# Down products in another order, with weight tiles made early and POOL left to begin transfers

## The chip, the cores and the metric

The kernel runs on one core of one Trainium2 chip. The metric is the device time of one execution in microseconds (us). TensorE is PE in the rows, VectorE DVE, ScalarE ACT, GpSimd POOL, and SyncE SP, which here only begins transfers.

## The reference, cut to what matters

Two blocks run one after the other on a 512 x 1024 activation; the change touches only the end of the second, its MLP and the final norm:

```python
u = _rmsnorm(h, mlp_norm_g[l])
h = h + jnp.square(jax.nn.relu(u @ w_up[l])) @ w_down[l]
...
h = _rmsnorm(h, final_norm_g)
return h[:, N_META:]
```

`w_up` is 1024 x 4096, `w_down` 4096 x 1024, all in float32.

## The kernel before

Each float32 operand is split into a high and a low half (`a_high` and `a_low` for activations, `hi` and `lo`), and PE sums high times high, low times high and high times low. ACT makes the high half of a weight tile (`cast`, a copy), DVE or POOL the low half (`w_low` on DVE, `low` on POOL, a subtraction each).

The MLP is cut into four parts of 1024 hidden columns. A part first has eight up tiles, each 24 matmuls on PE. The down product of the part is a Strassen-Winograd scheme: seven products instead of eight, named `P11`, `P_7`, `P_5`, `P12`, `P_6`, `P_3`, `P_4`, in the order of the numbers that the line `P11, P_7, ... = range(7)` gives them. Each takes an activation operand (a quarter or a signed sum of quarters, `x_sums`), and a weight operand (a quarter of `w_down` or a signed sum). Each weight operand has two tiles, h = 0 and 1; the fourteen tiles of a part are counted by i = 2n + h, n the product's number. The weight sums are made in `w12_w22` (`w_w` in the rows): SP loads a quarter, POOL begins DMA transfers that add further rows of `w_down` from DRAM (`w_sum`, `accum_op=ALU.add`): two tiles each for `P_7`, `P_5` and `P_6`, where the sum for `P_6` is put on top of that for `P_5`, and so begins only when the low halves of the two tiles of `P_5` are made. DVE adds the last term for `P_4` (`w_sum4`). The weights `w22`, one quarter without a sum, belong to `P_3`.

Every product fills two PSUM banks (r = 0, 1: rows 0 to 127 and 128 to 255 of an activation half), DVE empties them (`out`, in the last part `last_out`), and `down_free` says which emptying PE waits for before it fills banks again. `P_3` and `P_4` stay in PSUM over the parts. In the last part the sums over the products are spread over `OT`, the 512 x 1024 result in four row blocks, of which `y_half(1, 1)` (called y22) is the lower right quarter. Then the norm: ACT squares with a row sum (`square`), DVE makes mean and reciprocal, ACT the root, and DVE (`scale_left`) and ACT (`scale_right`) multiply; `times_g` multiplies by the gain `gl`. Each result block is stored as soon as it is scaled.

Each engine runs its list in the order in which its program writes it, and waits on semaphores only; the lists are written by hand. `raw` holds the weights as loaded for all tiles up to the last up tile. In the last part POOL makes the low halves of five second tiles (`P_5`, `P12`, `P_6`, `P_3`, `P_4`, h = 1) and, at the very end, finishes y22 and multiplies two blocks by the gain.

## Time and profile before

| what | us |
|---|---|
| median of 3 runs (1005.85 to 1006.09) | 1006.0 |
| the profiled execution | 1006.45 |
| its span, first to last instruction | 1004.7 |
| PE busy in the span | 983.4 |
| DVE busy in the span | 625.3 |
| POOL busy in the span | 552.3 |

The profile shows one execution. Busy time of PE counts overlapped matmuls; where the next matmul follows with no idle time in a timeline row, PE does not wait. A timeline row gives start, duration, engine, line and operation, what is written from what, how many instructions are merged, and in square brackets the idle time ahead and what ended it. Consecutive instructions of DVE overlap a little, so the distance of starts is what one costs.

### The profile page before, as it was taken

To read this page: it belongs to the slowest core of one execution; us is meant where nothing else is said; L and a number is where in the kernel's file an instruction comes from. 1 tells how busy PE (TensorE), PEld (TensorE's weight loads), DVE (VectorE), ACT (ScalarE), POOL (GpSimd) and SP (SyncE) were. 2 spreads that over 40 slices of the span, in tenths; PEclk is the share of its full clock that TensorE was granted. 3 is DMA by queue.
4 is the path that set the end of the run, shared out by engine and by line. 5 is a ranking of instruction groups with operands and counts; after the bars stand their busy time and mean duration, and the time that the engine had idled before them with its cause. 6 is when DMAs were issued, how large, how long until landed. Compare 5 with 4: busy or idle time off the path is not lost.

```text
span 1004.7 us, 12754 instructions
## 1 busy us (share of the span) xinstructions
PE 983.4 (98%) x4859; PEld 830.3 (83%) x4859; DVE 625.3 (62%) x943; ACT 471.8 (47%) x743; POOL 552.3 (55%) x643
## 2 busy tenths in 40 slices
PE   9999999999999999999999999999999999999993
PEld 7888788888888888888899987888888888888882
DVE  5781257665273753454669999773942852685698
ACT  4553345554672223533235775455633443453453
POOL 4555455565565884654657878455074055037084
PEclk9999999999999999999999999999999999999997
DMA  7323221212452225422232212568467458356122
GB/s 233 107 79 114 84 85 52 75 43 84 125 169 84 84 84 191 127 84 84 64 98 92 85 63 84 169 223 195 126 216 161 126 175 202 106 150 136 28 42 84
DMA packets 93276, 115.92 MB, mean 115 GB/s; under 512 B 3954, under 2 KB 70160, under 8 KB 93216
## 3 DMA queue, kind: packets, MB, share of 16 engines
q1 hardware_dynamic: 86384, 102.26, 31.3%
q0 software_dynamic: 6528, 12.58, 7.6%
q8 instruction: 38, 0.62, 0.3%
q10 hardware_dynamic: 304, 0.27, 0.1%
q14 instruction: 22, 0.18, 0.1%
HBM read 113.01 MB, written 2.10 MB: 115 GB/s over the span
## 4 chain that ended last, share of the span: by engine, by line
PE 87%; DVE 9%; ACT 2%; issue 2%; DVEq 0%; ACTq 0%
PE ps L565 63%; PE ps L958 12%; PE ps L584 4%; PE ps L710 1%; PE ps L634 1%; PE ps L731 1%; DVE Hl L1587 1%; PE ps L695 1%; PE ps L694 1%; PE ps L772 1%; PE ps L617 1%; DVE Fm L2334 0%; DVE Fm L2303 0%; DVE X L2389 0%; DVE tmp L2084 0%
## 5 line engine op out<-in xcount | busy, mean ns | idle before, releaser
L2470 POOL TENSOR_TENSOR wlo<-raw,whi 128x256 fp32r<-128x256 f32 x496 | 401.6, 860 | 215.4 <-ACT whi L1014 215.3
L565 PE MATMUL ps<-Hh,whi 128*128 128x512 f32 x512 | 201.8, 394 | 0.7 <-DVE Hl L1587 0.7
L565 PE MATMUL ps<-Hl,whi 128*128 128x512 f32 x512 | 199.6, 390 | 0.0
L1014 ACT ACTIVATE whi<-raw 128x1024 fp32r<-128x1024 f32 (+1 forms) x126 | 132.3, 1050 | 93.8 <-PE ps L565 54.0
L565 PE MATMUL ps<-Ah,whi 128*128 128x512 f32 (+1 forms) x496 | 165.3, 360 | 0.2 <-DVE Al L2238 0.2
L565 PE MATMUL ps<-Al,whi 128*128 128x512 f32 (+1 forms) x496 | 163.7, 356 | 0.0
L565 PE MATMUL ps<-Hh,wlo 128*128 128x512 f32 x512 | 129.3, 389 | 0.3 <-POOL wlo L2470 0.3
L565 PEld LDWEIGHTS ps<-Hh,whi 128*128 128x128 f32 x512 | 96.1, 188 | 20.9 <-DVE Hl L1587 1.5
L565 PEld LDWEIGHTS ps<-Hh,wlo 128*128 128x128 f32 x512 | 96.0, 188 | 20.7 <-POOL wlo L2470 0.7
L565 PEld LDWEIGHTS ps<-Hl,whi 128*128 128x128 f32 x512 | 96.2, 188 | 19.2
L565 PE MATMUL ps<-Ah,wlo 128*128 128x512 f32 (+1 forms) x496 | 104.7, 356 | 0.0
L565 PEld LDWEIGHTS ps<-Ah,whi 128*128 128x128 f32 x496 | 88.0, 188 | 13.7 <-DVE Al L2238 0.8
L565 PEld LDWEIGHTS ps<-Al,whi 128*128 128x128 f32 x496 | 87.9, 188 | 12.7
L565 PEld LDWEIGHTS ps<-Ah,wlo 128*128 128x128 f32 x496 | 83.3, 188 | 13.4
L2511 POOL DMA_DIRECT2D w_w<-in_w_down x20 | 24.3, 1217 | 117.1 <-DVE w_more L1587 53.0
L2270 DVE SCALAR_TENSOR_TENSOR X<-ps,Rb 128x512 f32<-128x512 f32 x32 | 21.8, 689 | 94.1 <-PE ps L565 93.3
L2481 POOL TENSOR_TENSOR P<-P,sm 128x1024 f32<-128x1024 f32 (+1 forms) x16 | 26.9, 1680 | 53.4 <-DVE sm L1779 53.4
L958 PE MATMUL ps<-whi,Hl 128*128 128x512 f32 x216 | 53.8, 390 | 0.1
L1590 DVE TENSOR_TENSOR tmp<-ps,Rb 128x512 f32<-128x512 f32 x25 | 17.2, 689 | 55.6 <-PE ps L565 55.6
L565 PE MATMUL ps<-Ah,w_more 128*128 128x512 f32 x160 | 50.2, 389 | 0.0
L958 PEld LDWEIGHTS ps<-whi,Hl 128*128 128x128 f32 x216 | 40.3, 188 | 9.4 <-issue 0.8
L2470 POOL TENSOR_TENSOR w_more<-raw,w_more 128x256 fp32r<-128x256 f32 x40 | 30.4, 925 | 18.0 <-ACT w_more L1014 18.0
(372 smaller groups left out, 1692.8 us busy)
## 6 DMA issues: line engine op xcount, KB each, us to landing
raw<-in_w_in SPq DMA_DIRECT2D x29, 1024.0 KB, 5.3
raw<-in_w_up SPq DMA_DIRECT2D x16, 1024.0 KB, 5.4
w_w<-in_w_down POOLq DMA_DIRECT2D x20, 512.0 KB, 5.8
Fm<-in_w_down SPq DMA_DIRECT2D x8, 1024.0 KB, 5.1
raw<-in_w_in SPq DMA_DIRECT2D x14, 512.0 KB, 3.7
raw<-in_w_att_out SPq DMA_DIRECT2D x4, 1024.0 KB, 5.1
raw<-in_w_sg_out SPq DMA_DIRECT2D x4, 1024.0 KB, 5.2
raw<-in_w_o SPq DMA_DIRECT2D x4, 1024.0 KB, 5.1
```

The costliest lines, as they stand in the source:

```text
L565: mm = e.matmul(ps[:, bk, 0:c1 - c0], of(j)[:, k % kk, 128 * g:128 * g + 128], x[:, k, c0:c1], start=(start and n == 0), stop=(stop and n ...
L584: mm = e.matmul(ps[:, banks[r], :], x[:, k, 128 * r:128 * r + 128], of(j)[:, k % 2], start=(i == 0 and n == 0), stop=(i == 3 and n == 5))
L617: e.matmul(ps[:, 2, 0:128], ones[:], ones[:], start=True, stop=True)
L634: mm = e.matmul(ps[:, i, :], of(i)[:, k], x[:, k], start=(k == 0 and of is w_hi and x is Hh), stop=last)
L694: e.matmul(out, lhs, kdh[:, g, k0:k0 + W], start=True, stop=False)
L958: mm = e.matmul(ps[:, down_bank(part, n, r), :], x[:, k, 128 * r:128 * r + 128], of(j)[:, k % 2], start=(first and not (kept and part)), s ...
L1014: return e.activation(out, src, ACT.Copy, scale=scale)
L1590: e.tensor_tensor(out, ps[:, bk, :], R, ALU.mult).then_inc(*b.done("drained", j))
L2270: e.scalar_tensor_tensor(X[:, n], ps[:, up_bank(part, n), :], 0.0, RB, ALU.max, ALU.mult).then_inc(*b.done("drained", j))
L2470: ins = e.tensor_tensor(w_lo(j)[:, *cut], raw_tile(j)[:, *cut], f(w_hi(j))[:, *cut], ALU.subtract)
L2481: e.tensor_tensor(Pf[:, u, :, :, 0:W], Pf[:, u, :, :, 0:W], rb, ALU.mult).then_inc(*b.done("probs", i))
L2511: e.dma_start(w_sum3[h] if n == P_7 else quarter(0, 1, h), src, accum_op=ALU.add).then_inc(*b.done(w_sum_name(n, h), (part, n), 16))
```

## The change

The numbers of `P12` and `P_5` are exchanged, in all four parts, and with them the order of their products on PE and of their tiles. In DVE's program the pieces between are put in another order. `raw` is allocated among the buffers of the first phases, and the new `w_last` over the same bytes: it holds high and low halves of the two tiles of `P_3` in the last part, which ACT and DVE now make while the last up tiles run. POOL makes no low half in the last down part: DVE makes all of them. `w_sum4` of the last part's second tile becomes an adding transfer that POOL begins, and so does the last addition on y22, from SBUF to SBUF. The multiplications by the gain of rows 256 to 511 (right half) go to DVE, and the left half of rows 0 to 255 is multiplied by gain and root in one instruction.

```diff
-P11, P_7, P_5, P12, P_6, P_3, P_4 = range(7)
+P11, P_7, P12, P_5, P_6, P_3, P_4 = range(7)
...
-        raw = sb("raw", [128, 2, 8, 256])
...
+            raw = first.enter_context(nc.sbuf_tensor("raw", [128, 2, 8, 256], F32))
...
+        w_last = sb("w_last", [128, 2, 2, 1024], R32)
...
+        def in_w_last(j):
+            return tiles[j][0] is None and tiles[j][1][:2] == (3, P_3)
+
+        def turn_of(j):
+            m = j - J_UP - 8
+            return m - 2 if j >= down_tile(3, P_4, 0) else m
+
         def w_place(part, j):
-            m = j - J_UP - 8
-            w = (whi, wlo)[part][:, (j if m < 0 else J_UP + 6 + m % 5) % 3].rearrange("p k n -> p (k n)")
-            if m >= 0 and m % 5 < 2:
+            m = turn_of(j)
+            if in_w_last(j):
+                w = w_last[:, tiles[j][1][2], part]
+            elif m >= 0 and m % 5 < 2:
                 w = w_more[:, m % 5, part]
+            else:
+                w = (whi, wlo)[part][:, (j if m < 0 else J_UP + 6 + m % 5) % 3].rearrange("p k n -> p (k n)")
...
-            if tiles[j][0] is not None:
-                return "lo", j
-            part, n, h = tiles[j][1]
-            return ("lo" if part == 3 and n >= P_5 and h == 1 else "w_low"), j
+            return ("w_low" if tiles[j][0] is None else "lo"), j
...
+                if n == P12 and part == 3:
                     return "first_kept", r
-                return "down_out", (part, {P_5: P11, P12: P_7, P_6: P_5}[n], r)
+                return "down_out", (part, {P12: P11, P_5: P_7, P_6: P12}[n], r)
...
                     else:
-                        w.wait_ge(*(("w_sum4", (part, h)) if n == P_4 else (w_sum_name(n, h), (part, n))))
-                m = j - J_UP - 8
-                before = j - 5 if m >= 2 else j - 3
-                if m in (0, 1):
+                        by_dve = n == P_4 and (part, h) != (3, 1)
+                        w.wait_ge(*(("w_sum4", (part, h)) if by_dve else (w_sum_name(n, h), (part, n))))
+                m = turn_of(j)
+                before = j - 3 if m < 2 else j - 5 if m == j - J_UP - 8 else j - 7
+                if in_w_last(j):
+                    w.wait_ge("lo", J_UP + 22 * 3 + 7)
+                elif m in (0, 1):
                     w.wait_ge("residual_turned", 7)
...
+                        if (part, n) == (3, 6):
+                            for h in range(2):
+                                cast(down_tile(3, P_3, h))
...
-                    if j < n_tiles:
+                    if i == 6:
+                        a_high(part, P_3)
+                    if i == 8:
+                        a_high(part, P_4)
+                    if j < n_tiles and not in_w_last(j):
                         cast(j)
-                    for n in {1: (P_5,), 2: (P12,), 4: (P_6,), 7: (P_3,), 8: (P_4,)}.get(i, ()):
-                        a_high(part, n)
-                    if part == 3 and i == 3:
+                    if i in (0, 2, 3):
+                        a_high(part, {0: P12, 2: P_5, 3: P_6}[i])
+                    if part == 3 and i == 2:
                         for r in range(2):
                             w.wait_ge("down_out", (3, P11, r))
...
-                if low_ready(j)[0] == "lo":
-                    return
...
+                b.value["vector_step", ("last", n)] = b.count["vector_step"]
...
                     if n == 6:
-                        for i in range(4):
+                        for i in (0, 1, 2, 3) if part < 3 else (0, 1, 2, 3, 10, 11):
                             w_low(part, i)
                 x_sums(part, P_5)
                 w_low(part, 4)
+                a_low(part, P12)
+                w_low(part, 5)
+                if part < 3:
+                    out(part, P11)
+                else:
+                    last_out(P11)
+                w_low(part, 6)
                 a_low(part, P_5)
-                w_low(part, 5)
-                send(P11)
                 x_sums(part, P_6)
-                w_low(part, 6)
-                a_low(part, P12)
-                send(P_7)
                 w_low(part, 7)
+                if part < 3:
+                    out(part, P_7)
+                else:
+                    last_out(P_7)
                 a_low(part, P_6)
                 w_low(part, 8)
                 x_sums(part, P_3)
                 w_sum4(part, 0)
-                send(P_5)
-                w_low(part, 9)
-                w_sum4(part, 1)
-                a_low(part, P_3)
-                w_low(part, 10)
-                w_low(part, 11)
-                w_low(part, 12)
-                a_low(part, P_4)
-                w_low(part, 13)
-                send(P12)
-                send(P_6)
+                if part < 3:
+                    out(part, P12)
+                    a_low(part, P_3)
+                    w_low(part, 9)
+                    w_sum4(part, 1)
+                    w_low(part, 10)
+                    w_low(part, 11)
+                    w_low(part, 12)
+                    a_low(part, P_4)
+                    w_low(part, 13)
+                    out(part, P_5)
+                    out(part, P_6)
+                else:
+                    last_out(P12)
+                    a_low(part, P_3)
+                    w_low(part, 9)
+                    w_low(part, 12)
+                    last_out(P_5)
+                    a_low(part, P_4)
+                    w_low(part, 13)
+                    last_out(P_6)
...
+                y = Z[:, r, 0:cut]
                 w.wait_ge("final_factor", r)
-                w.wait_ge(*(("first_times", r) if r < 2 else ("y22_times", r)))
-                w.wait_ge("last_times", r)
-                e.tensor_scalar(Z[:, r, 0:cut], Z[:, r, 0:cut], R4[:, r:r + 1], None, ALU.mult).then_inc(
-                    *b.done("scaled_left", r))
+                if r < 2:
+                    w.wait_ge("down_out", (3, P12, r))
+                    w.wait_ge("a_low", (3, P_4))
+                    e.scalar_tensor_tensor(y, OT[:, r, 0:cut], R4[:, r:r + 1], gl[:, 0:cut], ALU.mult, ALU.mult).then_inc(
+                        *b.done("scaled_left", r))
+                else:
+                    w.wait_ge("first_times", r)
+                    w.wait_ge("last_times", r)
+                    e.tensor_scalar(y, y, R4[:, r:r + 1], None, ALU.mult).then_inc(*b.done("scaled_left", r))
...
             w.wait_ge("down_out", (3, P_6, 1))
             add(y_half(0, 1), acc[3])
             add(y_half(1, 0), acc[3], ALU.subtract)
             w.wait_ge("final_g_in", 0)
-            for r in range(2):
-                times_g(r, 0, 512, "first_times", r)
+            w.wait_ge("a_low", (3, P_4))
             for r in range(2):
                 last_add(r, 0, down_bank(3, P_3, r), 512, 512)
-            for r in range(4):
+            for r in range(2):
                 first_mean(r)
             for r in range(2):
                 last_mean(r, 0)
             for r in range(2):
                 scale_left(r)
+            w.wait_ge("y22_set", 0)
+            for r in range(2, 4):
+                times_g(r, 512, 512, "first_times", r)
             last_add(2, 0, 6, 0, 512)
+            for r in range(2, 4):
+                first_mean(r)
             last_mean(2, 0)
             scale_left(2)
             last_add(3, 0, 7, 0, 256)
             add(OT[:, 3, 256:512], ps[:, 7, 256:512])
             last_mean(3, 0)
-            last_add(3, 1, down_bank(3, P12, 0), 256, 256)
+            last_add(3, 1, down_bank(3, P_5, 0), 256, 256)
             last_mean(3, 1)
             scale_left(3)
...
-                q, r = {P_7: (1, 1), P_5: (0, 0), P_6: (1, 1)}[n]
+                q, r = {P_7: (1, 1), P_5: (0, 0), P_6: (1, 1), P_4: (1, 0)}[n]
                 if n == P_7:
                     w.wait_ge("quarter7_in", (part, 1))
                 elif n == P_5:
                     w.wait_ge("quarter01_in", part)
                 else:
-                    w.wait_ge(*low_ready(down_tile(part, P_5, h)))
+                    w.wait_ge(*low_ready(down_tile(part, P_5 if n == P_6 else P_6, h)))
                 r0, c0 = 1024 * part + 512 * q + 256 * h, 512 * r
...
-                if part == 3:
-                    low(down_tile(3, P_5, 1))
                 w_sum(part, P_6, 1)
                 if part < 3:
                     lows(up_tile(part + 1, 0), up_tile(part + 1, 5))
-            for n in (P12, P_6, P_3, P_4):
-                low(down_tile(3, n, 1))
-
-            y = y_half(1, 1)
+            w_sum(3, P_4, 1)
             w.wait_ge("down_out", (3, P_6, 1))
-            e.tensor_tensor(y, y, acc[3], ALU.add).then_inc(*b.done("y22_set", 0))
-            w.wait_ge("y22_set", 0)
-            w.wait_ge("final_g_in", 0)
-            w.wait_ge("a_low", (3, P_4))
-            e.tensor_tensor(Z[:, 2, 512:1024], OT[:, 2, 512:1024], gl[:, 512:1024], ALU.mult).then_inc(
-                *b.done("y22_times", 2))
-            e.tensor_tensor(Z[:, 3, 512:1024], OT[:, 3, 512:1024], gl[:, 512:1024], ALU.mult).then_inc(
-                *b.done("y22_times", 3))
+            w.wait_ge("vector_step", ("last", P_5))
+            e.dma_start(y_half(1, 1), acc[3], accum_op=ALU.add).then_inc(*b.done("y22_set", 0, 16))
```

The bank and tile names in the waits of PE are exchanged likewise.

DVE in the first part, from the `out` of `P11` on. Low halves of weights read `hi`'s semaphore, `Hl` and `x_part` are low halves of activations, `tmp<-X` an activation sum, `w_w<-w_w,Fm` is `w_sum4`, and `Fm<-ps` an `out`. Before:

```order
L2314 COPY Fm<-ps 128x512 [waits s_products] x2
L2282 TENSOR_TENSOR tmp<-X,tmp 128x1024 [waits s_all_low]
L1587 TENSOR_TENSOR w_more<-Fm,w_more 128x1024 [waits s_hi]
L1587 TENSOR_TENSOR Hl<-X,Hl 128x1024 [waits s_all_high]
L2314 COPY Fm<-ps 128x512 [waits s_products] x2
L1587 TENSOR_TENSOR wlo<-Fm,whi 128x1024 [waits s_hi]
L1587 TENSOR_TENSOR Hl<-tmp,Hl 128x1024 [waits s_all_high]
L1587 TENSOR_TENSOR wlo<-w_w,whi 128x1024 [waits s_hi]
L2282 TENSOR_TENSOR tmp<-X,tmp 128x1024 [waits s_all_low]
L2292 TENSOR_TENSOR w_w<-w_w,Fm 128x1024 [waits s_all_low,s_quarter10_in]
L2314 COPY Fm<-ps 128x512 [waits s_products] x2
```

And now:

```order
L2331 COPY Fm<-ps 128x512 [waits s_products] x2
L1606 TENSOR_TENSOR w_more<-w_w,w_more 128x1024 [waits s_hi]
L1606 TENSOR_TENSOR Hl<-tmp,Hl 128x1024 [waits s_all_high]
L2301 TENSOR_TENSOR tmp<-X,tmp 128x1024 [waits s_all_low]
L1606 TENSOR_TENSOR wlo<-w_w,whi 128x1024 [waits s_hi]
L2331 COPY Fm<-ps 128x512 [waits s_products] x2
L1606 TENSOR_TENSOR Hl<-tmp,Hl 128x1024 [waits s_all_high]
L1606 TENSOR_TENSOR wlo<-w_w,whi 128x1024 [waits s_hi]
L2301 TENSOR_TENSOR tmp<-X,tmp 128x1024 [waits s_all_low]
L2311 TENSOR_TENSOR w_w<-w_w,Fm 128x1024 [waits s_all_low,s_quarter10_in]
L2334 TENSOR_TENSOR Fm<-ps,Fm 128x512 [waits s_residual_set,s_products]
```

The `out` ahead of the fifth product was that of `P_5`, and is now that of `P12` (the row with `s_residual_set`). The low half of tile 6 now stands right behind the `out` of `P11`: it is the first tile of `P_5`, the one that POOL's transfer for `P_6` waits for, and it was tile 4, above these rows, before.

POOL at the end of the program, before:

```order
L2511 DMA w_w<-in_w_down 128x2x512
L2511 DMA w_w<-in_w_down 128x2x512 [waits s_all_low]
L2470 TENSOR_TENSOR w_more<-w_w,w_more 128x2x128 [waits s_hi]
L2470 TENSOR_TENSOR w_more<-w_w,w_more 128x2x128 x3
L2511 DMA w_w<-in_w_down 128x2x512 [waits s_lo]
L2470 TENSOR_TENSOR wlo<-Fm,whi 128x2x128 [waits s_hi]
L2470 TENSOR_TENSOR wlo<-Fm,whi 128x2x128 x3
L2470 TENSOR_TENSOR w_more<-w_w,w_more 128x2x128 [waits s_hi]
L2470 TENSOR_TENSOR w_more<-w_w,w_more 128x2x128 x3
L2470 TENSOR_TENSOR wlo<-tmp,whi 128x2x128 [waits s_hi]
L2470 TENSOR_TENSOR wlo<-tmp,whi 128x2x128 x3
L2470 TENSOR_TENSOR wlo<-w_w,whi 128x2x128 [waits s_hi]
```

And now:

```order
L2554 DMA w_w<-in_w_down 128x2x512
L2554 DMA w_w<-in_w_down 128x2x512 [waits s_all_low] x3
L2613 DMA Fm<-Fm 128x2x512 [waits s_vector_step,s_down_out]
```

The rows of subtractions (two for each of the five tiles) are gone, and so are the addition and two multiplications behind them. Three adding transfers into `w_w` wait for DVE, and a fourth on `Fm` (y22) waits for the last `out`.

ACT at the end of the program; the first rows are the squares, the order of which the change leaves alone:

```order
L1569 ACTIVATE Fm,sm<-Fm 128x512 [waits s_down_out] x2
L1569 ACTIVATE Fm,sm<-Fm 128x512 [waits s_y22_set]
L1569 ACTIVATE Fm,sm<-Fm 128x512
L1569 ACTIVATE Fm,sm<-Fm 128x512 [waits s_last_added] x2
L1579 ACTIVATE sm<-sm 128x1 [waits s_all_inverse]
L1023 ACTIVATE X<-X,sm 128x512 [waits s_last_times,s_final_factor]
```

The squares of rows 256 to 511 (`s_y22_set`) stand ahead of those of the last-added columns of rows 0 to 255 (`s_last_added`). What sets `y22_set` was POOL's addition, and is now the end of the transfer.

## Rows read from the trace of the kernel before

**Rows 1.** The page, part 1: busy us, share of the span, instructions.

```profile
PE 983.4 (98%) x4859; PEld 830.3 (83%) x4859; DVE 625.3 (62%) x943; ACT 471.8 (47%) x743; POOL 552.3 (55%) x643
```

**Rows 2.** Timeline of PE, first part: start, duration, instruction, idle before.

```profile
725.14 1.07 PE L958 MATMUL ps<-wlo,Hl 128*128 128x512 f32 x4
726.27 2.09 PE L958 MATMUL ps<-whi,Hl 128*128 128x512 f32 x8
```

**Rows 3.** Timeline of DVE, first part.

```profile
709.99 1.22 DVE L1587 TENSOR_TENSOR wlo<-w_w,whi 128x1024 fp32r<-128x1024 f32 x1
...
716.30 1.22 DVE L1587 TENSOR_TENSOR w_more<-Fm,w_more 128x1024 fp32r<-128x1024 f32 x1
717.43 1.22 DVE L1587 TENSOR_TENSOR Hl<-X,Hl 128x1024 fp32r<-128x1024 f32 x1
...
725.44 1.28 DVE L2314 COPY Fm<-ps 128x512 f32<-128x512 f32 x2
```

**Rows 4.** Timeline of ACT, first part.

```profile
717.41 1.06 ACT L1014 ACTIVATE whi<-w_w 128x1024 fp32r<-128x1024 f32 x1 [2.90 <-DMA w_w<-in_w_down]
...
723.50 1.06 ACT L1014 ACTIVATE whi<-w_w 128x1024 fp32r<-128x1024 f32 x1 [4.09 <-DMA w_w<-in_w_down]
```

**Rows 5.** Timeline of POOL, first part, then third part.

```profile
711.62 1.20 POOL L2511 DMA_DIRECT2D w_w<-in_w_down  x1 [12.57 <-DVE wlo L1587]
717.72 1.21 POOL L2511 DMA_DIRECT2D w_w<-in_w_down  x1 [4.90 <-DVE w_more L1587]
...
872.20 1.21 POOL L2511 DMA_DIRECT2D w_w<-in_w_down  x1 [22.61 <-DVE wlo L1587]
879.11 1.22 POOL L2511 DMA_DIRECT2D w_w<-in_w_down  x1 [5.69 <-DVE w_more L1587]
```

**Rows 6.** DMA to landing, us: lines L2511 (POOL, adding), then L497 (SP).

```profile
DMA to landing us min/median/max: 5.5/5.8/6.6
...
DMA to landing us min/median/max: 3.3/4.6/5.5
```

**Rows 7.** Timeline of PE, last part.

```profile
949.44 2.88 PE L958 MATMUL ps<-w_more,Hl 128*128 128x512 f32 x12
...
971.27 2.29 PE L958 MATMUL ps<-whi,Hl 128*128 128x512 f32 x8
...
982.46 1.98 PE L1006 MATMUL ps<-whi,Hl 128*128 128x512 f32 x8
```

**Rows 8.** Timeline of DVE, last part.

```profile
949.64 0.69 DVE L2270 SCALAR_TENSOR_TENSOR X<-ps,Rb 128x512 f32<-128x512 f32 x1 [0.21 <-PE ps L565]
951.03 1.23 DVE L2282 TENSOR_TENSOR tmp<-X 128x1024 f32<-128x1024 f32 x1 [0.70 <-ACT X L1511]
...
975.33 1.76 DVE L1587 TENSOR_TENSOR w_more<-tmp,w_more 128x1024 fp32r<-128x1024 f32 x1
...
982.88 4.56 DVE L2303 TENSOR_TENSOR Fm<-Fm 128x1024 f32<-128x1024 f32 x2
987.48 3.33 DVE L2389 TENSOR_TENSOR X<-Fm,P 128x512 f32<-128x512 f32 x2
990.73 0.68 DVE L2400 TENSOR_TENSOR Fm<-ps,Fm 128x512 f32<-128x512 f32 x1
...
993.38 0.33 DVE L2394 TENSOR_SCALAR sm<-sm 128x1 f32<-128x1 f32 x4
...
995.51 0.68 DVE L2400 TENSOR_TENSOR Fm<-ps,Fm 128x512 f32<-128x512 f32 x1
```

**Rows 9.** Timeline of POOL, last part.

```profile
982.93 3.44 POOL L2574 TENSOR_TENSOR Fm<-Fm 128x1024 f32<-128x1024 f32 x1 [0.47 <-DVE Fm L2327]
```

**Rows 10.** Timeline of ACT, last part.

```profile
991.44 0.63 ACT L1550 ACTIVATE Fm<-Fm 128x512 f32<-128x512 f32 x1 [3.71 <-DVE Fm L2400]
991.98 0.19 ACT L1550 ACTIVATION_READ_ACCUMULATOR Fm<-Fm 128x1 f32 x1
...
1001.59 0.38 ACTq L1578 DMA_DIRECT2D out<-X  x1
```

More of the change, by code:

```diff
@@ L2344, in vector_program @@
             for part in range(4):
-                send = last_out if part == 3 else lambda n, part=part: out(part, n)
                 for n in range(8):
```

12 lines of the change are left out of this document (6 added, 6 removed).

## The prediction

> **What bounds the kernel now.** I read the page's busy times first: PE is busy 983.4 us [rows 1] of a span of 1004.7, so only two things can move the time: a wait of PE, or the stretch after its last matmul. Then PE's timeline around the down products. In the first part the fifth product, `P_6`, should start when the four matmuls of 725.14 are through. One costs (1.98 - 1.07) / 4 = 0.227 us, from eight and from four in a row [rows 2, 7], so that is at 726.05, and it starts at 726.27 [rows 2]: PE already waits 0.22 there, and the eight matmuls behind take 2.09, 0.11 more than the 1.98. DVE's row says for what: the `out` of `P_5`, begun at 725.44 [rows 3]. PE follows it by 0.83. One product costs 24 x 0.227 = 5.44.
>
> In the last part the down products start at 949.44, the fifth at 971.27 and the last stretch at 982.46 [rows 7]; PE ends near 988.2 by the same pitch (12 matmuls of 512 columns, 24 of 256). The span ends at 1004.7, so 16.5 us lie behind PE, and DVE's timeline says why: it begins the last two additions on `OT` at 982.88, the multiplications by the gain at 987.48, and reaches the products of rows 256 to 383 (`last_add(2, ...)`) only at 995.51 [rows 8]. From there to the issue of the last store is 6.08 [rows 10]. The end is DVE's list, up to 995.51 and then in turn with ACT. POOL makes part of its slowness: two additions take 4.56 beside POOL's of 3.44 [rows 8, 9], where an operation of that size costs 1.14 from start to start (716.30 to 717.43 [rows 3]); and subtractions as that of 975.33 take 1.76 instead of 1.22 [rows 8].
>
> **The change: DVE's work.** In the last part DVE gets five low halves more and gives up one `w_sum4`: +4 x 1.14 = 4.6 us, two of them ahead of the last `act`. Without POOL's subtractions it gets back about 0.54 on each of nine operations between 958 and 980, and 2.2 and 2.0 on the two pairs behind 982.88: 9.1 us. Two multiplications by the gain come (POOL's), two are merged into the scaling: 0.1 or so each. If DVE never waited, I count from the start of `act(3, 7)` 17 operations of 1.14, 14 of 0.60, two dependent additions of 1.25, four tail operations in 2.65 (990.73 to 993.38 [rows 8]), four of 0.60 and 2.6 of small ones and steps: 38 us, from 951.6 to 989.6, 5.9 before 995.51. That is what the change could give. I don't expect it, for the new waits.
>
> **The first part.** I walk DVE's new list from 709.99, where both lists have the low half of tile 4. Steps of 1.14 (the `out` pair 1.20): `a_low(P12)`, `w_low(5)`, `out(P11)` at 713.40, `w_low(6)` at 714.60. ACT's halves are there earlier. Before, POOL's first transfer for `P_6` was begun 1.63 after the start of `w_low(4)` (709.99 to 711.62 [rows 3, 5]); now it hangs on `w_low(6)`: 714.60 + 1.63 = 716.23, 4.6 later. What this delay was covered by: `cast(8)`, which started on landing at 717.41, 5.79 after the issue [rows 4, 5], while the tile's low half was made well after. Now `cast(8)` is at 722.02 and takes 1.06, `w_low(8)` is at 723.08, `x_sums(P_3)` and `w_sum4(0)` follow, and `out(P12)` at 726.50. PE waits for that `out`: fifth product at 726.50 + 0.83 = 727.33, 1.28 late instead of 0.22.
>
> The second transfer starts 6.10 after the first (711.62 to 717.72, with its condition met long before [rows 5]), at 722.33, and lands after 5.78 (717.72 to 723.50 [rows 4, 5]) at 728.11. Two ACT copies of about 1.0 (`cast(9)`, `a_high(P_3)`), then on DVE `a_low(P_3)` at 730.15 and only behind it `w_low(9)` at 731.29, through at 732.5. PE wants it after 20 of the product's 24 matmuls: 727.33 + 4.54 = 731.87. It waits 0.7. In all 1.98 instead of 0.33: **+1.6**, and 0.1 for `a_low(P_4)`, further back in the same list: +1.7. PE's time lost here is lost for good.
>
> **Second and third part.** There DVE is not behind at the start of the down products, and the first transfer would be begun at 876.81 instead of 872.20, `w_low(9)` ready near 893.2, wanted at 894.1. Margin 0.9 with a spacing of 6.1, and 0.1 with 6.91, which the third part's own transfers show [rows 5]. I take nothing; the upper bound is 0.8 for each.
>
> **The last part,** in before's clock. `w_low(3)` was through 0.21 ahead of `act(3, 7)` at 949.64; the two early tiles (2.27) push it to 951.62. The `x_sums` (951.03) starts at 953.01 [rows 8]. Then, with ACT's rows as before: `w_low(4)` 954.15, `w_low(6)` 958.77, first transfer 960.40; `last_out(P_7)`'s four operations 963.44, `w_low(8)` 967.25 (landing 966.19 and a copy), `last_out(P12)` 970.66, so PE's fifth product is at 971.49, 0.2 behind 971.27. Second transfer 966.50, landing 972.28, copies, `a_low(P_3)` 974.35, `w_low(9)` 975.49. PE waits for it from 976.03 to 976.80: 0.8. It moves PE's end to 988.9 and does not bound the end by itself. `w_low(9)` releases the third transfer (`w_sum(3, P_4, 1)`): 977.12, landing 982.9, copy, `w_low(13)` 984.0, `last_out(P_6)` 985.15. That releases the fourth, for y22: second operation at 985.75, its 0.68 [rows 8], and the 0.41 that POOL takes from the end of what it waits for to the issue (709.99 + 1.22 to 711.62): 986.84, landing 5.79 later at 992.63.
>
> Behind the wait for y22 on ACT stand four squares of 0.63 [rows 10] that all of DVE's means need: 992.63, 993.26, 993.89, 994.52. DVE has reached the means by 991.7 and waits. Both means and reciprocals stand ahead of `scale_left(0)`: the fourth square's sum is read 0.73 behind its start (991.44 to 991.98 + 0.19 [rows 10]), and two operations of 0.2 bring `scale_left(0)` to 995.65; four DVE operations of 0.60 follow, and `last_add(2, ...)` starts at 998.05, 2.54 behind 995.51. From there the list is the same but for two small means. **+2.5**.
>
> What is unknown here is a transfer from SBUF to SBUF. The adding transfers from DRAM land after 5.5 to 6.6, plain ones of the same 512 KB after 3.3 at the least [rows 6]. These are my bounds; I take 5.8, since it is the same adding operation of the same shape. With 3.3 all of the tail behind y22 comes 2.5 earlier: +0.05 in place of +2.5; with 6.6, +3.3.
>
> The page DMA: Bandwidth & Descriptors of the Trainium skill (its opening section on the chain of events of a transfer) gives about 2.0 us fixed and the bytes by 436 GB/s, and says that most of the fixed part is the receipt from the target memory, HBM the heaviest. By it 512 KB would take 3.2 us. The trace does not agree for adding transfers, whose least is 5.5 [rows 6], and no row here has one without DRAM.
>
> **Sum.** 1.7 + 2.5 = +4.2 on the span of 1004.7: 1008.9. The profiled execution took 1006.45, 1.75 more than its span, and stands 0.45 above the median. On the median: 1006.0 + 4.2 = **1010.2**.
>
> **Rivals.**
> *y22 lands quickly* (3.3): 1.7 + 0.05, 1007.8. For it: no DRAM read, no other transfer then. Against: all 24 adding ones need 5.5 or more. 0.18.
> *Transfers are spaced as in the third part* (6.91): 0.8 more in the first part, 0.8 in the last part's chain, and the thin margins of parts two and three begin to show: 1011.8 and up to 1013.5. For it: row 872.20 to 879.11. Against: loads of SP ran then, and none do in the last part. 0.12.
> *Faster: the chain of transfers does not bind.* Place: first and last part. Four transfers stand in a row in the last part, so each microsecond that one lands earlier gives up to four back, and two in the first part. At 5.1 from issue to landing both losses are gone (first part +0.3, last -0.3), and below it the 5.9 us of DVE come through: 1002 with 4.7, 1000.1 if nothing waits. For it: POOL no longer subtracts beside them. Against: in the first part it didn't either, and they took 5.78. 0.12.
> *Near no change by cover that I don't see* (an ACT copy that finds a gap, DVE's list shorter than walked): 1004 to 1008. 0.08.
>
> **Numbers.** The forecast has 0.50, for 1008.6 to 1011.5. The range, 1005.0 to 1013.5, leaves out the faster case and the far end of the wide spacing. A measurement of this kernel tells 0.2% (2 us) from no change: faster 0.12; same 0.17 (the last case and half of the quick y22); slower 0.71.
>
> **What would show it.** After: PE idle of about 1.2 and 0.7 at the fifth product and its second tile in the first part, and 0.8 in the last; no POOL subtraction behind 932; POOL's four transfers near 962, 968, 979 and 988.5, and 5.7 to 5.9 from each to its reader; an ACT gap of several microseconds that the y22 transfer ends, DVE idle behind it. Wrong: if ACT's squares start within 4 us of the last issue, if PE's first part shows no new wait, or if DVE is busy without a break up to `last_add(2, ...)`.

## Result, and the profile after

| kernel | median us | runs | profiled execution | its span |
|---|---|---|---|---|
| before | 1005.95 (1005.63 to 1006.09) | 7 | 1006.45 | 1004.7 |
| changed | 1009.04 (1008.4 to 1009.86) | 7 | 1009.45 | 1007.7 |

The ratio is 1.0033, with a 95% interval of 1.0024 to 1.0043: the change makes the kernel 3.1 us slower. The forecast was 1010.2, 4.2 slower.

The page, part 1, of the changed kernel answers to [rows 1]:

```profile
PE 983.2 (98%) x4859; PEld 829.6 (82%) x4859; DVE 630.6 (63%) x947; ACT 470.2 (47%) x743; POOL 532.4 (53%) x622
```

PE has the same work as before. DVE has 5.3 us more, POOL 19.9 less: nothing there says slower. The chain that ended last, part 4 of the page, does; the adding transfers, absent from this list before, are on it now:

```profile
PE 83%; DVE 10%; issue 2%; ACT 2%; DMA 2%; SPq 0%; DVEq 0%; POOLq 0%; ACTq 0%
PE ps L573 62%; PE ps L967 9%; PE ps L592 4%; PE ps L718 1%; DVE wlo L1606 1%; DMA w_w<-in_w_down 1%; PE ps L642 1%; PE ps L739 1%; DVE w_more L1606 1%; DVE Hl L1606 1%; PE ps L703 1%; PE ps L702 1%; DMA raw<-in_w_in 1%; PE ps L780 1%; DMA Fm<-Fm 0%
```

**First part.** The timeline of PE answers to [rows 2]. PE now waits for the `out` of `P12` (L2334) and for the low half of tile 9 (L1606):

```profile
724.39 1.07 PE L967 MATMUL ps<-wlo,Hl 128*128 128x512 f32 x4
726.75 2.08 PE L967 MATMUL ps<-whi,Hl 128*128 128x512 f32 x8 [1.29 <-DVE Fm L2334]
728.68 1.08 PE L967 MATMUL ps<-wlo,Hl 128*128 128x512 f32 x4
729.59 1.97 PE L967 MATMUL ps<-whi,Hl 128*128 128x512 f32 x8
731.84 1.21 PE L967 MATMUL ps<-wlo,Hl 128*128 128x512 f32 x4 [0.27 <-DVE wlo L1606]
732.89 2.46 PE L967 MATMUL ps<-w_more,x_part 128*128 128x512 f32 x10
```

Behind each wait stand an ACT copy of a tile that a transfer fills, and the transfer. POOL, then ACT, then DVE, same stretch; they answer to [rows 3 to 5]:

```profile
715.47 1.20 POOL L2554 DMA_DIRECT2D w_w<-in_w_down  x1 [17.06 <-DVE w_more L1606]
721.73 1.21 POOL L2554 DMA_DIRECT2D w_w<-in_w_down  x1 [5.05 <-DVE Hl L1606]
```

```profile
721.42 1.06 ACT L1023 ACTIVATE whi<-w_w 128x1024 fp32r<-128x1024 f32 x1 [2.86 <-DMA w_w<-in_w_down]
727.38 1.06 ACT L1023 ACTIVATE whi<-w_w 128x1024 fp32r<-128x1024 f32 x1 [4.91 <-DMA w_w<-in_w_down]
```

```profile
722.51 1.23 DVE L1606 TENSOR_TENSOR wlo<-w_w,whi 128x1024 fp32r<-128x1024 f32 x1 [1.59 <-ACT whi L1023]
...
725.92 1.28 DVE L2334 TENSOR_TENSOR Fm<-ps,Fm 128x512 f32<-128x512 f32 x2
729.42 1.22 DVE L1606 TENSOR_TENSOR x_part<-tmp,x_part 128x1024 fp32r<-128x1024 f32 x1 [2.22 <-ACT x_part L1023]
```

The reader sees one chain: transfer at 715.47, copy at 721.42 (5.95 later), low half of tile 8, a sum, `w_sum4(0)`, then the `out` that PE waits for. The copy of the next tile is 5.65 behind its own transfer.

**Last part.** The timelines of POOL, ACT and DVE answer to [rows 8 to 10]:

```profile
961.49 1.22 POOL L2554 DMA_DIRECT2D w_w<-in_w_down  x1 [23.92 <-DVE wlo L1606]
967.58 1.22 POOL L2554 DMA_DIRECT2D w_w<-in_w_down  x1 [4.88 <-issue]
978.08 1.21 POOL L2554 DMA_DIRECT2D w_w<-in_w_down  x1 [9.28 <-DVE w_more L1606]
987.58 1.22 POOL L2613 DMA_DIRECT2D Fm<-Fm  x1 [8.29 <-DVE Fm L2344]
```

```profile
983.65 1.06 ACT L1023 ACTIVATE whi<-w_w 128x1024 fp32r<-128x1024 f32 x1 [6.43 <-DMA w_w<-in_w_down]
...
992.62 0.63 ACT L1569 ACTIVATE Fm<-Fm 128x512 f32<-128x512 f32 x1 [6.69 <-DMA Fm<-Fm]
...
1004.59 0.38 ACTq L1597 DMA_DIRECT2D out<-X  x1
```

```profile
954.11 1.23 DVE L2301 TENSOR_TENSOR tmp<-X 128x1024 f32<-128x1024 f32 x1 [0.70 <-ACT X L1523]
...
984.74 1.23 DVE L1606 TENSOR_TENSOR wlo<-w_w,whi 128x1024 fp32r<-128x1024 f32 x1 [2.36 <-ACT whi L1023]
...
987.20 2.48 DVE L2320 TENSOR_TENSOR Fm<-Fm 128x1024 f32<-128x1024 f32 x2
...
994.60 0.16 DVE L2443 SCALAR_TENSOR_TENSOR sm<-sm 128x1 f32<-128x1 f32 x1 [2.01 <-ACT Fm L1569]
...
998.02 0.68 DVE L2433 TENSOR_TENSOR Fm<-ps,Fm 128x512 f32<-128x512 f32 x1
...
999.98 0.16 DVE L2443 SCALAR_TENSOR_TENSOR sm<-sm 128x1 f32<-128x1 f32 x1 [0.42 <-DVE sm L2427]
```

The two additions take 2.48 instead of 4.56 [rows 8], so DVE is faster where POOL is silent, and it gives the time back waiting for ACT, which waits for transfers. The y22 transfer's own entry says how long it took:

```profile
L2613 POOL DMA_DIRECT2D Fm<-Fm x1: 1223/1223/1223, 987.6 to 987.6; - x1
...
DMA to landing us min/median/max: 5.0/5.0/5.0
```

**One yardstick for all kernels.** The rows give four stretches that add up to the path from the first down product to the last issue: A, from PE's `P11` in the first part to `P11` in the last; B, from there to DVE's `x_sums` (954.11 above, 951.03 in [rows 8]); C, from there to `last_add(2, ...)`; D, from there to the last issue.

| kernel | A | B | C | D | sum |
|---|---|---|---|---|---|
| before | 245.15 | 1.59 | 44.48 | 6.08 | 297.30 |
| changed | 247.01 | 3.56 | 43.91 | 6.57 | 301.05 |
| changed, a second profile | 246.59 | 3.56 | 43.90 | 6.56 | 300.61 |

A starts at 704.29 before and at 703.54 after; between profiles of all the kernels below it lies anywhere from 703.0 to 704.4, ahead of the down products. That is why the sum grows by 3.75 and the span by 3.0. C is the stretch where the change could gain, and it hardly moved: 0.6 less, for 2.0 more in B, where DVE makes the two early tiles. The idle times in DVE's rows within C say why. They were 1.43 in sum and are 7.16 (2.36 and 2.01 are the two shown above whole); C without them fell from 43.05 to 36.75. It is 36.7 to 37.2 in every kernel below in which DVE has the same operations in C and POOL is silent, so there C differs by DVE's waits and by little else.

### The profile page after: what moved, and what is told of

The parts are those of the page before. It is cut to its first block, busy times and chain, and to the rows that moved or that the text cites. A ratio compares the mean times of both kernels' runs of the same rounds, so it can differ in the third digit from the quotient of the medians.

```text
span 1007.7 us, 12730 instructions
## 1 busy us (share of the span) xinstructions
PE 983.2 (98%) x4859; PEld 829.6 (82%) x4859; DVE 630.6 (63%) x947; ACT 470.2 (47%) x743; POOL 532.4 (53%) x622
## 4 chain that ended last, share of the span: by engine, by line
PE 83%; DVE 10%; issue 2%; ACT 2%; DMA 2%; SPq 0%; DVEq 0%; POOLq 0%; ACTq 0%
PE ps L573 62%; PE ps L967 9%; PE ps L592 4%; PE ps L718 1%; DVE wlo L1606 1%; DMA w_w<-in_w_down 1%; PE ps L642 1%; PE ps L739 1%; DVE w_more L1606 1%; DVE Hl L1606 1%; PE ps L703 1%; PE ps L702 1%; DMA raw<-in_w_in 1%; PE ps L780 1%; DMA Fm<-Fm 0%
## 5 line engine op out<-in xcount | busy, mean ns | idle before, releaser
L2513 POOL TENSOR_TENSOR w_more<-raw,w_more 128x256 fp32r<-128x256 f32 x40 | 34.5, 994 | 13.5 <-ACT w_more L1023 13.5
```

What stands on the lines that cost most here:

```text
L2513: ins = e.tensor_tensor(w_lo(j)[:, *cut], raw_tile(j)[:, *cut], f(w_hi(j))[:, *cut], ALU.subtract)
```

## Experiments

Twelve experiments in three groups; the kernel before ran beside each group (medians 1005.94, 1006.1 and 1006.17). The stretches are those of one profiled execution each, the medians those of 5 to 11 executions. All compute the whole reference. Edits are against the changed kernel where nothing else is said; the stretches of all of them are in a table at the end of this section.

### Two causes in the tail

`squares_first`: ACT squares the last-added columns of rows 0 to 255 and scales them ahead of the two squares that need y22 (`first_square(r)` stands for the wait and the square of one row block).

```diff
-            for r in range(4):
+            for r in range(2):
                 first_square(r)
             for r in range(2):
                 last_square(r, 0, 512, 512)
             for r in range(2):
                 scale_right(r)
+            for r in range(2, 4):
+                first_square(r)
```

> The changed kernel with ScalarE's squares of the last-added columns of rows 0 to 255, their roots and scalings put ahead of the two squares that wait for the y22 transfer. If that wait is what holds VectorE's means (2.0 us idle ahead of them in the changed kernel's trace), the means start near 992.6 instead of 994.6 and last_add(2) near 995.8 instead of 998.0: 2.2 us faster than the changed kernel, about 1006.8. If the end is bound by VectorE's own list or by the transfer's landing in another way, no change beyond 0.5 us.

1006.69 (1005.88 to 1007.03), ratio 1.0007 [0.9998, 1.0016]. C falls from 43.91 to 41.36: 2.55, a little more than the 2.01 and 0.26 that DVE waited for ACT's squares (the rest are slightly shorter waits for landings). Nothing in ACT's timeline waits for the y22 transfer any more, and DVE goes on behind its small products:

```profile
991.74 0.21 DVE L2432 TENSOR_SCALAR sm<-sm 128x1 f32<-128x1 f32 x2
991.99 0.16 DVE L2448 SCALAR_TENSOR_TENSOR sm<-sm 128x1 f32<-128x1 f32 x1
```

`y22_on_dve`: DVE makes the y22 addition, first of three, and there is no transfer.

```diff
+            w.wait_ge("vector_step")
+            e.tensor_tensor(y_half(1, 1), y_half(1, 1), acc[3], ALU.add).then_inc(*b.done("y22_set", 0))
             add(y_half(0, 1), acc[3])
...
-            w.wait_ge("down_out", (3, P_6, 1))
-            w.wait_ge("vector_step", ("last", P_5))
-            e.dma_start(y_half(1, 1), acc[3], accum_op=ALU.add).then_inc(*b.done("y22_set", 0, 16))
```

> The changed kernel with the last addition on y22 made by VectorE ahead of its two others, in place of the transfer. Theory of the transfer: ScalarE's squares start near 988.5 instead of 992.6, VectorE pays 1.25 for the addition and loses no 2.0 in waiting, last_add(2) 0.7 to 0.9 earlier, about 1008.2. Rival (VectorE's list is the bound and the transfer hidden): 1.2 us slower than the changed kernel, about 1010.2.

1007.21 (1006.54 to 1007.83), 1.0012 [1.0003, 1.0021]. C is 42.52, 1.39 less: the wait is gone and 1.15 of DVE work is in its place. D falls by 0.37 too, which was not expected: the step of 0.42 ahead of the mean is gone, behind the same two small operations (the mean starts at 998.18, 0.25 behind the first of them, and 0.63 behind it in the changed kernel). No run shows why.

`y22_on_pool`: the addition as it was before, an operation of POOL.

```diff
-            e.dma_start(y_half(1, 1), acc[3], accum_op=ALU.add).then_inc(*b.done("y22_set", 0, 16))
+            e.tensor_tensor(y_half(1, 1), y_half(1, 1), acc[3], ALU.add).then_inc(*b.done("y22_set", 0))
```

> The changed kernel with the last addition on y22 back on GpSimd, as before, in place of the transfer. It is ready about 3.4 us after its start against 5.0 for the transfer, but VectorE's two additions beside it slow down from 2.5 to 4.6 us as before the change; VectorE's idle 2.0 ahead of the means takes that in. Theory: the two cancel, within 0.5 us of the changed kernel. Rival (the transfer's landing alone decides): 1.6 us faster.

1010.0 (the middle one of 1009.0, 1009.74, 1010.0, 1010.04 and one execution of 2005.91, which is out of line with every other), 1.0035 [1.0021, 1.0048]. C is 44.09. DVE no longer waits ahead of its means, and its two additions are slow again, beside POOL's:

```profile
987.80 3.40 POOL L2613 TENSOR_TENSOR Fm<-Fm 128x1024 f32<-128x1024 f32 x1 [8.24 <-DVE Fm L2344]
```

```profile
987.74 4.53 DVE L2320 TENSOR_TENSOR Fm<-Fm 128x1024 f32<-128x1024 f32 x2
```

The slow pair costs 2.05 and the waits for the squares behind the transfer 2.27, so both mechanisms are real and nearly cancel. Expected was a time within 0.5 of the changed kernel; it is 0.7 above the one of its group by the medians and 0.04 to 0.48 by the sums of the stretches, so a small gain from the transfer can't be excluded (the four executions without the one of 2005.91 have 1009.9 in their middle).

### The order of DVE's list

`out_p12_early`: in the first three parts DVE empties the banks of `P12` ahead of the low half of tile 8, and makes that of tile 9 ahead of `a_low(P_3)`.

```diff
                 a_low(part, P_6)
+                if part < 3:
+                    out(part, P12)
                 w_low(part, 8)
                 x_sums(part, P_3)
                 w_sum4(part, 0)
                 if part < 3:
-                    out(part, P12)
-                    a_low(part, P_3)
                     w_low(part, 9)
+                    a_low(part, P_3)
```

> The changed kernel with two moves in VectorE's list of the first three parts: the emptying of P12 ahead of the low half of tile 8, and the low half of tile 9 ahead of the activation low half of P_3. If the first part loses its 1.9 us because these two stand behind the adding transfers' landings, TensorE's waits of 1.29 and 0.27 there go and the kernel is 1.5 us faster than the changed one, about 1007.5. Rival (the loss comes from the exchange of the products itself, or shows up as another wait): no change.

1007.05 (1006.23 to 1008.18), 1.001 [1.0001, 1.0019]. A is 244.94, 2.07 less than in the changed kernel's first profile, 1.65 less than in its second, and 0.21 less than before. The timeline of PE has no wait left at the fifth product or in it:

```profile
724.77 1.98 PE L967 MATMUL ps<-whi,Hl 128*128 128x512 f32 x8
726.59 1.07 PE L967 MATMUL ps<-wlo,Hl 128*128 128x512 f32 x4
727.50 1.99 PE L967 MATMUL ps<-whi,Hl 128*128 128x512 f32 x8
729.32 1.07 PE L967 MATMUL ps<-wlo,Hl 128*128 128x512 f32 x4
```

DVE itself still idles 2.29 us there for the second tile; it only no longer has work queued behind the wait that PE needs. So the transfers are late, and PE paid because of what stood behind them in DVE's list. The margin is thin: in `all_three`, with the same list there, the second tile's copy starts 5.70 behind its issue instead of 5.48, and PE starts its matmuls 0.25 late.

`last_tile9_first`: the same exchange in the last part alone.

```diff
                     last_out(P12)
-                    a_low(part, P_3)
                     w_low(part, 9)
+                    a_low(part, P_3)
```

> The changed kernel with one move in the last part: the low half of tile 9 ahead of the activation low half of P_3. If the last part's end hangs on the chain of adding transfers, the third and fourth are begun 1.1 us earlier, TensorE's wait of 0.36 goes too, and the kernel is about 1.1 us faster than the changed one, about 1007.9. Rival (the chain is covered by VectorE's own work): at most 0.3 us.

1006.88 (1006.41 to 1007.52), 1.001 [1.0001, 1.0019]. C is 41.48, 2.4 less, about twice what was expected. The exchange is worth one operation of 1.14 on DVE, and the ACT copy `a_high(P_3)` too, which runs behind that of tile 9 and for which DVE waited as well (2.30 at 975.36 in the changed kernel's timeline). The third transfer is now 2.68 behind the start of the copy of tile 9, and was 4.77; the expectation counted the operation of 1.14 and left out the copy, which is the other 0.95. Counted from the first transfer it is 14.21, and was 16.59; 0.29 of that are shorter landings:

```profile
961.99 1.21 POOL L2554 DMA_DIRECT2D w_w<-in_w_down  x1 [25.55 <-DVE wlo L1606]
...
976.20 1.21 POOL L2554 DMA_DIRECT2D w_w<-in_w_down  x1 [7.12 <-DVE w_more L1606]
```

`changed_again`: the changed kernel once more, in the second group, as a control.

> The changed kernel once more, as the reference of this group. In the last group the second adding transfer of the first part was begun 5.8 us after the first, in the changed kernel's own profile 6.26. If that is the chip and not the edits, this run can lie anywhere from 1007.5 to 1009.1, with TensorE's wait in the first part near 0.8 if the distance is 5.8 and near 1.3 if it is 6.2.

1009.31 (1008.84 to 1009.92), 1.0031 [1.0019, 1.0043]. The size of the loss is the same as in the first measurement. The two transfers of the first part start 5.84 apart, and PE's wait is 0.87: near the first of the two cases expected, but at the slow time of the second. The landing in the first part alone does not set the time.

`all_three`: `squares_first`, `out_p12_early` and `last_tile9_first` together.

> The changed kernel with the three moves together: the squares first, the emptying of P12 and the tile-9 low half early in the first three parts, and the tile-9 low half first in the last. If the losses add up (2.0 at the end, 1.3 to 1.6 in the first part, 1.0 in the chain), it is 4 us under the changed kernel of this group and 1.5 to 2.5 us under the kernel before: about 1004. Rival (the losses hide one another, the end then waits for TensorE or VectorE's list): 1005.5 to 1006.

1004.15 (1003.73 to 1005.38), 0.9982 [0.9973, 0.9991]: faster than before. The three medians alone fell by 2.35, 1.99 and 2.16 against 1009.04, 6.5 in sum; together they give 4.9 to 5.2. C is 40.22 and A 245.32. DVE waits 3.07 in C, where the waits saved by `squares_first` and `last_tile9_first` alone (2.76 and 2.53 of 7.16) would leave 1.87. Of the 1.2 between, 0.7 are landings: the second and third transfer's copies start 5.98 and 5.90 behind their issues, and 5.67 and 5.51 in `last_tile9_first`.

### The distance between two transfers

The second transfer's condition (the low half of tile 7) is met early, and yet it starts some 6 us behind the first. The rows above say when: 721.73 is 0.31 behind ACT's copy at 721.42, which starts when the first transfer has landed, and 967.58 is 0.31 behind the copy at 967.27.
```diff
-    nc = _bacc.Bacc("TRN2", target_bir_lowering=False, num_devices=1, dynamic_dma_scratch_size=1024)
+    nc = _bacc.Bacc("TRN2", target_bir_lowering=False, num_devices=1, dynamic_dma_scratch_size=1856)
```

1006.23 (1005.57 to 1006.83), 1.0002 [0.9993, 1.0011]: all of the loss, 3.1 against `changed_again` in the same group, is gone with one number. POOL's timeline, last part:

```profile
960.12 1.21 POOL L2554 DMA_DIRECT2D w_w<-in_w_down  x1 [32.17 <-DVE wlo L1606]
963.73 1.20 POOL L2554 DMA_DIRECT2D w_w<-in_w_down  x1 [2.40 <-DVE wlo L1606]
974.13 1.22 POOL L2554 DMA_DIRECT2D w_w<-in_w_down  x1 [9.20 <-DVE w_more L1606]
983.67 1.22 POOL L2613 DMA_DIRECT2D Fm<-Fm  x1 [8.32 <-DVE Fm L2344]
```

The second is now 3.61 behind the first and not the 1.2 that the expectation named, since its condition is met only then: its idle time ends with DVE's `wlo`, the low half of tile 7, where the row of the changed kernel had "issue". In the first part DVE starts the low halves of tiles 6 and 7 3.53 apart, and the transfers follow 3.55 apart. (The changed kernel's row of the first part, 721.73, names DVE's `Hl`. It is not the condition: with the larger room the transfer starts at 718.51, before that operation.) C is 41.31. PE still waits 1.07 for the `out` of `P12` in the first part, since that hangs on the first transfer.

`before_1856`: the same number in the kernel before.

> The kernel before with the same larger room. There the fifth product waits for the emptying of P_5 and not for a tile of the sums, and the second transfer of a part lands well before it is wanted, so earlier transfers have nothing to give: 1006.0, within 0.5. Rival: the larger room helps every kernel of this family by some 3 us, as it did the changed one; then 1003.

1005.78 (1005.11 to 1006.52), 0.9998 [0.9989, 1.0007]. Its stretches are those of before within 0.06. In the first part the second transfer starts 2.86 behind the first instead of 6.10, and nothing comes of it. In these kernels the room helps only where a tile of the sums is waited for.

`all_three_1856`: the three moves and the room.

> The three moves together left DVE three waits in the last part, of 1.59, 0.49 and 0.99 us, each for an ACT copy of a tile that an adding transfer fills. The first two hang on the second transfer, which began 5.95 behind the first although its condition (the low half of tile 7) was met long before. With more room for POOL's descriptors it began 3.6 behind in the changed kernel. If the two causes are separate, the first two waits go (2.1 us) and the third stays, because its transfer hangs on the low half of tile 9 and comes earlier by as much as DVE does: 1004.15 - 2.1 = 1002.0. The rival is that both edits remove the same wait: then 1004 or no better than 1003.5.

1001.62 (1001.4 to 1002.34), 0.9959 [0.9947, 0.9972]: the fastest of all, 4.5 us below the kernel before and 7.4 below the changed one (7.7 below `changed_again`; the changed kernel did not run in this group). C is 38.43, 1.8 less than in `all_three` where 2.1 was expected, and A is 0.5 less, which was not: PE's late start at the second tile of the fifth product in the first part is gone too. So the time expected, 1002.0, came out partly by luck. Between its `x_sums` and the means DVE has one wait of 0.26 and this one, for the third transfer:

```profile
978.90 1.23 DVE L1611 TENSOR_TENSOR wlo<-w_w,whi 128x1024 fp32r<-128x1024 f32 x1 [1.30 <-ACT whi L1023]
```

### What POOL's work costs beside DVE

`all_y22_on_dve_1856`: `all_three_1856` with the y22 addition on DVE, the edit of `y22_on_dve`.

> The first kernel of this call with the last addition on y22 made by DVE instead of a transfer. With the squares of rows 0 to 255 first, the landing of the transfer is behind nothing, so the transfer hides the addition fully, and DVE's list gets 1.25 us longer ahead of all the final scaling: 1.2 slower than the first kernel. Rival: the landing still binds somewhere behind the scaling of rows 0 to 255; then 0.5 slower or less.

1002.52 (1002.07 to 1002.9), 0.9967 [0.9955, 0.998]: 0.9 slower by medians of five executions each, 0.34 by the sums of the stretches. The low half of tile 13, ahead of the edit, starts 0.41 earlier behind the last part's `x_sums` in this profile, which the edit can't cause. From there to `last_add(2, ...)` DVE takes 1.12 more, and D shrinks by 0.36: the edit costs 0.76. `y22_on_dve` against `squares_first` gives nearly the same (1.16 in C, 0.37 back in D). Once its landing is off the path, the transfer is the better place, by about 0.8; the 1.2 expected left out what D gives back.

`tile7_on_pool_1856`: `all_three_1856` with one low half of the last part, that of tile 7, made by POOL between its first two transfers (DVE's `w_low` leaves that tile out, and the readers wait for POOL's semaphore).

```diff
                 w_sum(part, P_6, 0)
+                if part == 3:
+                    low(down_tile(3, P_5, 1))
                 w_sum(part, P_6, 1)
```

> The first kernel of this call with one low half, that of tile 7 in the last part, given back to POOL between its first and its second transfer. DVE saves 1.14 us; POOL needs four operations of about 0.86, and in these 3.4 us three of DVE's subtractions take 1.76 instead of 1.22, 1.6 in all. If the price of sharing is what the rows before showed, the time is 0 to 0.8 above the first kernel. Rival: DVE's own 1.14 is worth more than the slowing, then 0.5 or more faster.

1003.36 (1002.92 to 1004.13), 0.9976 [0.9967, 0.9985]: 1.7 slower, about twice the upper end of what was expected. POOL, then DVE:

```profile
959.54 3.30 POOL L2521 TENSOR_TENSOR wlo<-w_w,whi 128x256 fp32r<-128x256 f32 x4
```

```profile
959.59 4.34 DVE L2306 TENSOR_TENSOR tmp<-X,tmp 128x1024 f32<-128x1024 f32 x1
```

One DVE operation of 1.22 lasts 4.34: it started 0.05 behind POOL's and stood still until POOL's four were through (962.84). It lost 3.1 us, nearly all of POOL's time, to save 1.14. The kernel before has a milder case: DVE starts a subtraction at 963.79, while POOL's four run until 964.89, and it lasts 2.18, so that 1.1 of it lie before POOL's end. POOL, then DVE, before:

```profile
961.60 3.29 POOL L2470 TENSOR_TENSOR wlo<-Fm,whi 128x256 fp32r<-128x256 f32 x4
```

```profile
963.79 2.18 DVE L1587 TENSOR_TENSOR Hl<-tmp,Hl 128x1024 fp32r<-128x1024 f32 x1
```

The section "SBUF: two separate sides" of the page SBUF — State Buffer of the Trainium skill says that GpSimd and a VectorE operation with two SBUF inputs share one pair of ports, which whoever starts first holds for a whole instruction, so that the other is blocked and not slowed in part. The row of 4.34 agrees, and more strongly: the DVE operation didn't get in between POOL's four instructions either. In [rows 8] the same kind of operation shows 1.76, a smaller loss, which the rule by itself doesn't size, and no run shows what decides between the two.

### The stretches of all kernels

| kernel | A | B | C | D | sum |
|---|---|---|---|---|---|
| squares_first | 246.38 | 3.56 | 41.36 | 6.57 | 297.87 |
| y22_on_dve | 246.62 | 3.57 | 42.52 | 6.20 | 298.91 |
| y22_on_pool | 246.87 | 3.56 | 44.09 | 6.57 | 301.09 |
| out_p12_early | 244.94 | 3.56 | 43.28 | 6.57 | 298.35 |
| last_tile9_first | 246.71 | 3.56 | 41.48 | 6.57 | 298.32 |
| all_three | 245.32 | 3.56 | 40.22 | 6.56 | 295.66 |
| scratch_1856 | 246.15 | 3.56 | 41.31 | 6.57 | 297.59 |
| before_1856 | 245.14 | 1.59 | 44.42 | 6.08 | 297.23 |
| all_three_1856 | 244.80 | 3.56 | 38.43 | 6.56 | 293.35 |
| all_y22_on_dve_1856 | 244.80 | 3.55 | 39.14 | 6.20 | 293.69 |
| tile7_on_pool_1856 | 244.80 | 3.56 | 40.23 | 6.41 | 295.00 |

## Why the prediction was right, step by step

**First part, +1.7: measured +1.86.** The fifth product starts 23.21 behind `P11` (703.54 to 726.75) and started 21.98 behind it before (704.29 to 726.27, [rows 2]): +1.23, predicted +1.06. The sixth starts 29.35 behind (732.89), before 27.55: +1.80, predicted +1.6. The two waits are where the prediction had them, for the named operations. PE's first idle time is 1.29 for a predicted 1.2. The second is 0.27 in its row for a predicted 0.7, but the 12 matmuls from 729.59 take until 732.89, which is 0.58 more than 12 x 0.227. `out_p12_early`, which takes these two operations out from behind the landings, gives 1.65 to 2.07 back. The spacing of the transfers was 6.26 for a predicted 6.10. The size varies with one thing: in the six profiles with the same list and room in the first part, PE's first idle time is 0.82 to 1.29, and it is each time 4.64 to 4.66 less than the time from the first transfer's issue to its copy (5.47 to 5.95). A without the two idle times is 245.4 to 245.6 in all six.

**Second and third part, nothing: right.** A row of the second part's down products starts 1.11 later than before (787.35 against 786.24), and so does the last part's `P11` (950.55 against 949.44): nothing is lost between.

**Last part, +2.5 up to `last_add(2)`: measured +1.40.** The changed profile's last part runs 1.11 behind before's, so 1.11 is taken off. First transfer 960.38 (predicted 960.40), `x_sums` 953.00 (953.01), second transfer 6.09 behind the first (6.10), third 976.97 (977.12). PE starts the fifth product at 971.50 (971.49) and waits 0.36 for tile 9 (0.8). Two terms were too large. The third transfer was issued 0.15 earlier than predicted and its copy started 5.57 behind it and not 5.78, so the y22 transfer was issued at 986.47 instead of 986.84: 0.37. And the y22 transfer, taken at 5.8 with bounds of 3.3 and 6.6, was read 5.04 behind its issue: 0.75. Together 1.12, the whole difference. Its nearest row was taken to be an adding transfer of the same size from DRAM. The transfer from SBUF to SBUF lies between the two groups of [rows 6]: 0.5 under the shortest adding one there, 0.4 over the median of the plain ones (4.6).

**Behind it, nothing: measured +0.5.** D grows from 6.08 to 6.57. "The list is the same but for two small means" took these means at nothing. Together they are 0.21 long and stand between the last product and the mean that needs the newest sum, and that mean starts only after a step of 0.42 that DVE waits for itself (the row at 999.98). The misses have opposite signs, 1.1 too much in the chain and 0.5 too little behind it, and part of the number's closeness is that they cancel: on the path from the first down product on it is 3.75 for a predicted 4.2.

**The page's figure.** By the page DMA: Bandwidth & Descriptors of the Trainium skill 512 KB would take 3.2 us. The y22 transfer, which has no DRAM at either end, took 5.0 in all nine profiles that have one. The page's fit does not hold for adding transfers here.

**The rivals.** *y22 lands quickly*: it landed 0.75 earlier than taken, of the 2.5 that this rival needed. *Wide spacing*: refuted, 5.78 to 6.26 in the first and last part of every profile of the changed lists with the small room, and 5.87 in the third part of the changed kernel, where the kernel before had its 6.91. *Faster, the chain does not bind*: refuted for this kernel. Its price was near: for a DVE that never waits the prediction put `last_add(2, ...)` at 989.6, 40.16 behind the last part's `P11` at 949.44. In `all_three_1856` it is 41.99 behind (948.15 to 990.14), with 1.56 of DVE's waits behind `x_sums` in it, where before has 46.07 (B + C). *Near no change by cover*: refuted; no operation of ACT or DVE was found that hides the landings.

So the change does what it is built for: it frees DVE of POOL. In the last part its loss is a chain of four transfers: the first hangs on DVE's low half of tile 6, the second on the landing of the first, the third and the fourth on work of DVE behind a tile that the transfer ahead fills; and in the queues of PE, ACT and DVE work stands behind the operations that wait for a landing. In the first part the first two links are enough. `scratch_1856` and `squares_first` break the chain at different places and take away 3.1 and 2.4. That each would gain was expected from that theory, and so was the size for `squares_first` (2.2). Not settled: how much of the 1.3 to 1.6 that the three moves together fall short of their sum is shared, and how much is that the transfers of one profile land later than those of another; and where the step of 0.42 in D comes from.

## What to carry to other kernels

When work moves from a slow engine to transfers, count the transfers in a row and ask what stands behind each reader in its queue; here 3 us were lost with POOL 19.9 us less busy, PE the same and DVE only 5.3 us busier, and more than won back by four moves in two engines' lists. Put the reader of a late transfer last among independent work, on both the engine that reads it and the one that waits for that.
## What was not expected of the hardware

- With a room of 1024 bytes the second of two adding transfers of 512 KB by POOL starts 0.31 or 0.32 us behind the reader of the first, 5.78 to 6.26 behind the first itself, and with 1856 when its own condition is met, 3.54 to 3.61 behind (2.86 in the kernel before, 4.49 where POOL has work between). A price shows in the same profiles: with the larger room the longest landing in a profile is 9.4 to 10.5 us behind the issue, and 6.0 to 6.9 with the small one. The medians are 5.7 to 5.9 and 5.5 to 5.8.
- An adding transfer of 512 KB from SBUF to SBUF takes 5.0 us, an adding one from DRAM 5.4 at the least over all profiles, a plain one in the kernel before 3.3 at the least.
- POOL's four subtractions held one operation of DVE for 3.1 us, though earlier rows had shown 0.54 for each of several. DVE's operation had started 0.05 us behind POOL's first, and the rows don't show what made the loss small elsewhere.
